# Mixing and memory attention of tokens 0 to 511 moved into the sparse units, and a fourth tile counted by ScalarE

## The chip, the cores and the metric

One core of one Trainium2 chip runs the whole kernel. The metric is the device time of one execution in microseconds (us); the number compared is the median of several executions.

## The reference, cut to what matters

One decoder layer over 1024 tokens of width 1024: a projection feeds a sparse attention (8 heads; each query keeps the 256 keys with the highest index score) and a banded attention (8 heads); their joint output is mixed with x, goes through cross attention over 256 memory tokens, and through a squared ReLU MLP, with a layer norm behind each.

```python
rel = jax.nn.relu(einsum('bthd,bsd->bths', iqb, ik))
score = einsum('bths,bth->bts', rel, iwb) * idx_scale
score = where(causal, score, -inf)
_, sel = lax.top_k(score, n_sel)             # 256 keys of each query
...
x = LN(ALPHA * x + concat(sparse, band) @ w_o)                 # mixing
x = LN(ALPHA * x + memory_cross_attention(x, mem, wq, wk, wv, wo))
x = LN(ALPHA * x + square(relu(x @ w_up)) @ w_down)            # MLP
```

## The kernel before, in words

Every fp32 product is done as three products of rounded halves: high by high, high by low, low by high (lines 651 to 653). Weights come in chunks of 128 x 2048: SP (SyncE's queue) loads a chunk into one of two buffers `raw` (L610), and POOL makes its two halves, `w_hi` (L637, four instructions of 128x512) and `w_lo` (L642, four). The program is written out by hand: each engine has its own list, and semaphores tie the lists together. In PE's order the stages are

- the projection of the values, then 28 rope halves (24 matmuls each, L651 to L653), which make queries and keys; beside halves 15 to 20 stand the index scores of tiles 2 to 7 (a tile is 128 tokens). DVE rotates each half and splits it (`roped`), ScalarE rounds and stores it;
- the band stage, 40 steps of `swa_scores`, `swa_turn` and `swa_values`, with products over the memory tokens between them (`memory_product`; the keys and values of the memory, folded into `g_dram` and `u_dram`);
- the sparse units: 48 of them, tiles 2 to 7 by 8 heads, one new unit a step. Unit d is `scores(d)` (L703, L704), two steps later `turn_probs` (L831), and one step after that `times_values` (L844). Unit d of tile i needs the key mask of tile i;
- 48 products of mixing and memory attention, g = 0 to 47, each 24 matmuls of 128x512: g 0 to 15 mixing (weights `w_o`), 16 to 31 the scores of the memory attention (weights `g_dram`), 32 to 47 its output (weights `u_dram`). The eight tiles t follow one another for each half of the columns. Behind most products the result of an earlier tile is transposed (`turn_result`, L853, 8 transposes), and DVE does the norm or the probabilities of an earlier product;
- the MLP, up and down.

The search for each tile's 256th highest score is a bisection over 31 bits. The narrow tiles 2, 3 and 4 are counted by DVE (`tally`, L1483); the three wide tiles 5, 6 and 7 by ScalarE (`count_wide`, L1047), 5 bits beside the last rope halves and the rest beside band stage and first units; then DVE makes the masks (`finish`, L1563 to L1581). `select_for(us)` lets DVE take as much of the search as a budget allows at each step.

The weights of the mixing products lie in four slots: `slot_of(c)` is `c % 2` below `C_MIX` and `(c - C_MIX) % 4` from there, so POOL converts chunk c as soon as chunk c - 4 is used. Each pair of chunks serves 8 products. `load_queries` (L528, 8 DMAs) brings the queries of a tile, three tiles at most in buffers.

Of the kernel before, what the change touches and what calls it, by code (L numbers as in the profile page):

```python
# [62 lines left out]
C_G = C_MIX + 4  # L63
C_U = C_G + 4
C_MLP = C_U + 4
# [15 lines left out]
def rope_units():  # L81

    units = [(C_K, ("k", 0), hf) for hf in range(2)]
    for chunk, what in ((C_IQ, "iq"), (C_SQ, "sq"), (C_DQ, "dq")):
        for m in range(2):
            units += [(chunk + m, (what, m), hf) for hf in range(2)]
    return units
# [6 lines left out]
INDEX_HALF = 2 * N_ROPE_INDEX + 3  # L94
BESIDE_HALF = INDEX_HALF + (NT - FIRST_TOPK_TILE)
WIDE_HALF = BESIDE_HALF + 1
# [10 lines left out]
IDX = [(i, h) for i in range(FIRST_TOPK_TILE, NT) for h in range(HEADS)]  # L107
# [26 lines left out]
L_ATT = 0  # L134
L_GEMM = L_ATT + ND
L_DOWN = L_GEMM + 3 * 2 * NT
T_SWA = 0
T_DSA = []
_n = T_SWA + NS
for _i, _h in DSA:  # L140
    T_DSA.append(_n)
    _n += (_i + 4) // 4
T_O = _n
T_STAGE = T_O + 2 * NT

N_SEL = NT - FIRST_TOPK_TILE
WIDE = N_SEL - 3
# [4 lines left out]
WIDE_END = N_HALVES - 2  # L153

def wide_bit_beside_rope(v):

    return TOP_BIT - (v - WIDE_HALF) if WIDE_HALF <= v < WIDE_END else None

def wide_bit_counted(n):

    done = WIDE_END - WIDE_HALF
    j = (4 * n + 6) // 7
    return TOP_BIT - done - j if n >= 0 and 7 * j // 4 == n and j <= TOP_BIT - done else None

MEM_STEP = 2
BUDGET_BAND, BUDGET_DSA = 1.8, 2.0
FIRST_PRODUCT = 3  # L170
# [21 lines left out]
def last_uses():  # L192
# [7 lines left out]
    for n in range(12):  # L200
        stage, ch = divmod(n // 2, 2)
        last[C_MIX + n] = ("L", L_GEMM + 16 * stage + 8 * ch + NT - 1)
# [8 lines left out]
N_GEMM = 3 * 2 * NT  # L211

def transposed_at(g):

    stage, t = divmod(g - NT - 2, 2 * NT)
    return (stage, t) if 0 <= stage < 3 and 0 <= t < NT else None

def build_layer(nc, a):  # L220
# [6 lines left out]
    with ctx:  # L227
# [9 lines left out]
        w_at = [16, 32, 80, 96]  # L237
        w_hi = [place(f"w_hi{s}", [P, CHUNK], F32R, w_at[s]) for s in range(4)]
        w_lo = [place(f"w_lo{s}", [P, CHUNK], F32R, w_at[s] + 8) for s in range(4)]
# [29 lines left out]
        act_hi = place("act_hi", [P, NT, NK, P], F32R, 112)  # L269
        act_lo = place("act_lo", [P, NT, NK, P], F32R, 144)  # L270
# [6 lines left out]
        band_prob = [place(f"band_prob{s}", [P, PAIR * BAND], F32, 183 + 2 * s) for s in range(4)]  # L277
        kv_hi = [place(f"kv_hi{s}", [P, 2, MEM], F32R, 191 + 4 * s) for s in range(2)]
        kv_lo = [place(f"kv_lo{s}", [P, 2, MEM], F32R, 193 + 4 * s) for s in range(2)]
# [18 lines left out]
        unread_wide = [place(f"unread_wide{s}", [P, SEQ], BF16, 60 + 4 * s) for s in range(3)]  # L298
# [5 lines left out]
        p_store = place("p_store", [P, NT, HALF], F32, 176.5)  # L304
        gamma = place("gamma", [P, D], F32, 192.5)
        beta = place("beta", [P, D], F32, 196.5)
        x_res = [place(f"x_res{s}", [P, HALF], F32, 200.5 + 2 * s) for s in range(2)]
        p_work = [place(f"p_work{s}", [P, HALF], F32, 200.5 + 2 * s) for s in range(2)]
# [35 lines left out]
        unread_banks = [banks[:, (2 + 2 * s) * HALF:(4 + 2 * s) * HALF] for s in range(3)]  # L344
# [58 lines left out]
        q_split = sem("q_split")  # L403
        qk_stored = sems("qk_stored", 2)
        keys_in = sem("keys_in")
# [53 lines left out]
        def raw_of(c):  # L459

            return c if c < C_MEM else c + 1

        def mem_raw(slot_view=raw[C_MEM % 2]):

            return slot_view[:].rearrange("p (k m) -> p k m", k=NK)
# [5 lines left out]
        def slot_of(c):  # L471
            return c % 2 if c < C_MIX else (c - C_MIX) % 4
# [4 lines left out]
        def source_of(c):  # L477
# [6 lines left out]
            if c < C_G:  # L484
                return a["w_o"][c - C_MIX]
            if c < C_MLP:
                dram = g_dram if c < C_U else u_dram
                ch, kh = divmod((c - C_G) % 4, 2)
                return dram[4 * kh:4 * kh + 4, :, ch * HALF:(ch + 1) * HALF].rearrange("k p n -> p k n")
# [7 lines left out]
        def _(sp):  # L497
            def load_gb(n):
                sp.dma_start(gamma[:], a["gamma"][n].partition_broadcast(P)).then_inc(gb_in, 16)
                sp.dma_start(beta[:], a["beta"][n].partition_broadcast(P)).then_inc(gb_in, 16)  # L500

            def load_queries(j):

                if j < NT - FIRST_TOPK_TILE:
                    row, i = HEAD_ROW["iq"], FIRST_TOPK_TILE + j
                    units = N_ROPE_INDEX
# [7 lines left out]
                if j >= 3:  # L514
# [6 lines left out]
                    else:  # L521
                        filled(sp, l_full, L_ATT + (before - N_BAND) * HEADS + HEADS - 1)
# [14 lines left out]
            def load_keys():  # L537

                for s in range(2):
                    sp.wait_ge(qk_stored[s], 64)  # L540
                for j in range(4):
                    for part, key in enumerate((key_hi[j], key_lo[j])):
                        for d0 in range(0, P, ROT):
                            r0 = d0 % HEAD // ROT * P + j * ROT
                            sp.dma_start(key[d0:d0 + ROT, :].bitcast(F32),
# [753 lines left out]
        def _(dve):  # L1299
# [162 lines left out]

            def select_keys():

# [523 lines left out]
```

## Time and profile before

| | |
|---|---|
| median of 3 executions | 1640.76 us (1640.23 to 1644.03) |
| the profiled execution, its time | 1633.94 us |
| its span on the core | 1632.1 us |
| mean granted clock of TensorE | 0.970 of full speed |
| PE busy, matmuls | 1513.5 us (93% of the span) |
| DVE, ScalarE, POOL busy | 892.2, 465.4, 536.1 us |

The stages by the profiled execution: projection of the values to 35.9 us, rope halves to 239.6, band stage to 452.8, sparse units to about 610, mixing and memory attention to 925, MLP to 1632.1.
### The profile page before, as it was taken

To read this page: it belongs to the slowest core of one execution; us is meant where nothing else is said; L and a number is where in the kernel's file an instruction comes from. 1 tells how busy PE (TensorE), PEld (TensorE's weight loads), DVE (VectorE), ACT (ScalarE), POOL (GpSimd) and SP (SyncE) were. 2 spreads that over 40 slices of the span, in tenths; PEclk is the share of its full clock that TensorE was granted. 3 is DMA by queue.
4 is the path that set the end of the run, shared out by engine and by line. 5 is a ranking of instruction groups with operands and counts; after the bars stand their busy time and mean duration, and the time that the engine had idled before them with its cause. 6 is when DMAs were issued, how large, how long until landed. Compare 5 with 4: busy or idle time off the path is not lost.

```text
span 1632.1 us, 20732 instructions
## 1 busy us (share of the span) xinstructions
PE 1513.5 (93%) x7720; PEld 1286.1 (79%) x7720; DVE 892.2 (55%) x1819; ACT 465.4 (29%) x987; POOL 536.1 (33%) x540
## 2 busy tenths in 40 slices
PE   7999975888768999989999999999999999999996
PEld 6887754888757998768887788888888888888884
DVE  7568986778877433593426733333333333333357
ACT  3014435788674651122211201111101011111010
POOL 5232214665510003341233153333333333333300
PEclk9999997999887999999999999999999999999998
DMA  6564223554410004211110221111111110111001
GB/s 224 178 190 149 94 100 127 179 173 151 141 46 16 12 7 168 97 42 49 52 53 0 78 78 52 52 52 52 52 52 52 52 52 29 49 52 52 1 26 78
DMA packets 61331, 128.96 MB, mean 79 GB/s; under 512 B 6960, under 2 KB 34096, under 8 KB 53552
## 3 DMA queue, kind: packets, MB, share of 16 engines
q1 hardware_dynamic: 44208, 100.37, 18.6%
q10 hardware_dynamic: 17024, 27.27, 4.7%
q8 instruction: 62, 1.02, 0.3%
q14 instruction: 37, 0.30, 0.1%
HBM read 100.35 MB, written 27.26 MB: 78 GB/s over the span
## 4 chain that ended last, share of the span: by engine, by line
PE 77%; DVE 14%; ACT 3%; issue 3%; POOL 1%; DMA 1%; ACTq 0%; SPq 0%; DVEq 0%; POOLq 0%
PE banks L651 22%; PE banks L653 22%; PE banks L652 22%; PE banks L844 3%; PE banks L703 2%; PE banks L704 2%; DVE unread L1483 2%; PE banks L831 2%; ACT unread_wide L1047 2%; PE banks L853 1%; DVE h_buf L1792 1%; DVE bn L1778 1%; PE banks L800 1%; DVE trial L1460 1%; DVE h_buf L1801 1%
## 5 line engine op out<-in xcount | busy, mean ns | idle before, releaser
L637 POOL TENSOR_SCALAR w_hi<-raw 128x512 fp32r<-128x512 f32 x268 | 174.5, 677 | 1011.9 <-PE banks L653 685.0
L642 POOL TENSOR_TENSOR w_lo<-raw,w_hi 128x512 fp32r<-128x512 f32 x268 | 363.9, 1389 | 0.0
L1892 DVE TENSOR_TENSOR h_buf<-h_buf,banks 128x1024 f32<-128x1024 f32 x112 | 136.7, 1221 | 145.8 <-PE banks L653 145.8
L651 PE MATMUL banks<-act_hi,w_hi 128*128 128x512 f32 x512 | 200.0, 391 | 1.7 <-DVE act_lo L1771 1.7
L651 PE MATMUL banks<-w_hi,hid_hi 128*128 128x512 f32 x512 | 199.3, 389 | 1.4 <-DVE hid_lo L1872 1.4
L653 PE MATMUL banks<-act_hi,w_lo 128*128 128x512 f32 x512 | 199.9, 390 | 0.0
L652 PE MATMUL banks<-act_lo,w_hi 128*128 128x512 f32 x512 | 199.7, 390 | 0.0
L653 PE MATMUL banks<-w_hi,hid_lo 128*128 128x512 f32 x512 | 199.2, 389 | 0.0
L652 PE MATMUL banks<-w_lo,hid_hi 128*128 128x512 f32 x512 | 199.2, 389 | 0.0
L1263 ACT ACTIVATE relu_buf<-banks 128x512 f32<-128x512 f32 x64 | 38.3, 599 | 523.4 <-PE banks L653 523.4
L1867 DVE TENSOR_TENSOR relu_buf<-relu_buf 128x512 f32<-128x512 f32 x64 | 45.0, 704 | 241.9 <-ACT relu_buf L1263 241.9
L651 PE MATMUL banks<-w_hi,act_hi 128*128 128x512 f32 x384 | 152.6, 397 | 0.0
L653 PE MATMUL banks<-w_hi,act_lo 128*128 128x512 f32 x384 | 150.1, 391 | 0.0
L652 PE MATMUL banks<-w_lo,act_hi 128*128 128x512 f32 x384 | 149.9, 390 | 0.0
L651 PEld LDWEIGHTS banks<-act_hi,w_hi 128*128 128x128 f32 x512 | 96.5, 189 | 22.0 <-issue 1.9
L651 PEld LDWEIGHTS banks<-w_hi,hid_hi 128*128 128x128 f32 x512 | 96.1, 188 | 21.8 <-DVE hid_lo L1872 1.9
L652 PEld LDWEIGHTS banks<-act_lo,w_hi 128*128 128x128 f32 x512 | 96.5, 189 | 20.1
L653 PEld LDWEIGHTS banks<-act_hi,w_lo 128*128 128x128 f32 x512 | 96.4, 188 | 20.1
L652 PEld LDWEIGHTS banks<-w_lo,hid_hi 128*128 128x128 f32 x512 | 96.1, 188 | 20.0
L653 PEld LDWEIGHTS banks<-w_hi,hid_lo 128*128 128x128 f32 x512 | 96.1, 188 | 20.0
L703 PE MATMUL banks<-key_hi,q_tile 128*128 128x512 f32 (+3 forms) x240 | 88.1, 374 | 23.5 <-DVE neg_max L1690 8.7
L651 PE MATMUL banks<-x_hi,w_hi 128*128 128x512 f32 x224 | 89.3, 398 | 10.0 <-DVE roped L1377 7.3
(178 smaller groups left out, 2779.6 us busy)
## 6 DMA issues: line engine op xcount, KB each, us to landing
raw<-w_up_dram SPq DMA_DIRECT2D x16, 1024.0 KB, 4.8
raw<-w_down_dram SPq DMA_DIRECT2D x16, 1024.0 KB, 4.8
q_tile<-qk_dram SPq DMA_DIRECT2D x176, 64.0 KB, 2.1
qk_dram<-q_hi ACTq DMA_DIRECT2D x28, 256.0 KB, 2.2
qk_dram<-roped ACTq DMA_DIRECT2D x28, 256.0 KB, 2.6
x_raw<-x_t_dram SPq DMA_DIRECT2D x8, 512.0 KB, 8.4
raw<-wk_mem_dram SPq DMA_DIRECT2D x4, 1024.0 KB, 5.4
raw<-wv_mem_dram SPq DMA_DIRECT2D x4, 1024.0 KB, 5.2
```

Source lines behind the costliest of these rows:

```text
L637: pool.tensor_scalar(w_hi[s][:, col], raw[r % 2][:, col], 1.0, 1.0, ALU.mult, ALU.mult)\
L642: pool.tensor_tensor(w_lo[s][:, col], raw[r % 2][:, col], w_hi[s][:, col].bitcast(F32), ALU.subtract).then_inc(w_ready, 1)
L651: pe.matmul(dst, lh, rh, start=(first and n == 0), stop=False)
L652: pe.matmul(dst, lh, rl, start=False, stop=False)
L653: last = pe.matmul(dst, ll, rh, start=False, stop=(final and n == len(parts) - 1))
L703: pe.matmul(dst[:, lo:hi], q, key_hi[key][:, k0 + lo:k0 + hi], start=True, stop=False)
L704: mm = pe.matmul(dst[:, lo:hi], q, key_lo[key][:, k0 + lo:k0 + hi], start=False, stop=True)
L831: mm = pe.transpose(ring_t[m % 2][:, (j % 4) * P:(j % 4 + 1) * P], prob[d % 2][:, j * P:(j + 1) * P], ident[:])
L844: mm = pe.matmul(ring_a[m % 2][:, h * HEAD:(h + 1) * HEAD], prob_t[d % 2][:, j * P:(j + 1) * P], v_all[:, j, HEADS:HEADS + HEAD], start=(j ...
L1263: act.activation(relu_buf[q % 2][:], ring_a[(A_UP + q) % 2][:], ACT.Relu)\
L1867: dve.tensor_tensor(relu_buf[q % 2][:], relu_buf[q % 2][:], relu_buf[q % 2][:], ALU.mult)\
L1892: dve.tensor_tensor(h_buf[:, t, :], h_buf[:, t, :], ring_l[n % 2][:], ALU.add)\
```

## The change

Tokens 0 to 511 (tiles 0 to 3, called group 0) no longer wait for the later tiles. Their 24 products stand among the steps: g0 at step 49, g1 at step 53 (in the units of tiles 2 and 3), g2 to g8 in a row at step 59, and g9 to g23 at steps 60, 62, 65, 68, 71, 74, 76, 79, 82, 85, 88, 90, 93, 94 and 94, among the units of tiles 4 to 7 (steps 60 to 91). `GAP` leaves steps 56 to 59 without a new unit. Group 1, tiles 4 to 7, has its own 24 products behind. Each pair of chunks now serves 4 products instead of 8, so the 12 chunks of weights are loaded and converted a second time for group 1 (`C_LATE`). Up to `C_LATE` the chunks have only two slots, since the sparse units hold the room of the others.

```diff
-C_G = C_MIX + 4
-C_U = C_G + 4
-C_MLP = C_U + 4
+GROUP = 4
+C_LATE = C_MIX + 12
+C_MLP = C_LATE + 12
...
+GAP = 4
+N_STEPS = NS + ND + GAP
+def unit_at(n):
+    d = n - NS
+    if d >= 2 * HEADS:
+        d = d - GAP if d >= 2 * HEADS + GAP else -1
+    return d if d < ND else -1
+def step_of_product(g):
+    if g < 2:
+        return NS + HEADS + 1 + 4 * g
+    if g < 9:
+        return NS + 2 * HEADS + 3
+    return min(NS + 2 * HEADS + GAP + 28 * (g - 9) // 10, N_STEPS + 2)
...
         def slot_of(c):
-            return c % 2 if c < C_MIX else (c - C_MIX) % 4
+            return c % 2 if c < C_LATE else (c - C_LATE + 2) % 4
...
-                if 2 <= c < C_MIX + 2:
+                if 2 <= c < C_LATE:
                     chunk_used(pool, c - 2)
-                elif C_MIX + 2 <= c < C_MIX + 4:
+                elif C_LATE <= c < C_LATE + 2:
                     attended(pool, 2 * NT - 1)
+                    chunk_used(pool, C_MIX + 9)
-                elif c >= C_MIX + 4:
+                elif c >= C_LATE + 2:
                     chunk_used(pool, c - 4)
...
-            for n in range(NS + ND + 3):
+            for n in range(N_STEPS + 3):
                 if n < NS:
                     swa_scores(n)
-                elif n < NS + ND:
-                    scores(n - NS)
+                if unit_at(n) >= 0:
+                    scores(unit_at(n))
...
+                for g in products_of_step(n):
+                    for key in first_turned(0) if g == 0 else ():
+                        turn(*key)
+                    product(0, g)
```

The selection changes too. Tile 4 is now counted by ScalarE with tiles 5 to 7, tile by tile: 6 bits beside rope halves 22 to 27, 16 in the band stage, 4 at steps 41, 46, 51 and 56, and 5 behind products g2 to g6; DVE counts tiles 2 and 3 alone. For that, index scores of tiles 2 and 3 move to halves 10 and 11 and of tiles 7, 6, 5, 4 to halves 15 to 18, and the first part of the selection of each tile is spread over halves 12, 13 and 19 to 22. POOL takes the low half (`roped` minus its rounding) of the last seven rope pairs from DVE. The memory tokens have a buffer of their own and are rounded beside the last rope half, and that half is rotated at step 2. `act_hi`, `p_store`, `gamma` and others become two buffers, one for each group.

```diff
-WIDE = N_SEL - 3
+WIDE = N_SEL - 4
...
-WIDE_HALF = BESIDE_HALF + 1
+INDEX_HALVES = {10: 2, 11: 3, 15: 7, 16: 6, 17: 5, 18: 4}
+PREPARE_HALVES = {12: 2, 13: 3, 19: 7, 20: 6, 21: 5, 22: 4}
+WIDE_HALF = 22
+POOL_SPLIT = 7
...
+COUNT_TICKS = [("step", 3 + 37 * j // N_STEP_BITS) for j in range(N_STEP_BITS)]
+COUNT_TICKS += [("step", NS + n) for n in (1, 6, 11, 16)] + [("product", g) for g in range(2, WIDE_LEFT - 18)]
...
+                if c == C_MEM:
+                    indexed(sp, i_full, len(IDX) - 1)
+                    sp.dma_start(mem_raw[:], a["mem_t"]).then_inc(mem_in, 16)
+                if C_MEM + 2 < c < C_MIX + 2:
+                    ahead = 3 + tile_at(mem_unit(c - 3) - 1)
+                else:
+                    ahead = {C_MIX + 2: NT + 6, C_MIX + 4: NT + 7, C_MIX + 6: NT + 8}.get(c, 0)
```

First place: the queue of SP about the loads of the mixing weights (a wait on `w_ready` is a wait for POOL to have converted chunk c - 2; the wait on `l_full` of a query load is one for the scores of the last unit that read the buffer). Before, all queries are ahead of the first wait for a mixing weight:

```order
L528 DMA q_tile_86<-qk_dram 32x4x128 x7
L528 DMA q_tile_84<-qk_dram 32x4x128 [waits l_full1,qk_stored1,qk_stored0]
L528 DMA q_tile_84<-qk_dram 32x4x128 x7
L499 DMA gamma<-gamma_dram 128x1024 [waits stored1,a_full1,stored0]
L500 DMA beta<-beta_dram 128x1024
L610 DMA raw_50<-w_o_dram 128x2048 [waits w_ready]
L610 DMA raw_49<-w_o_dram 128x2048 [waits w_ready]
L610 DMA raw_50<-g_dram 128x4x512 [waits w_ready]
L610 DMA raw_49<-g_dram 128x4x512 [waits w_ready]
```

After, the queries of tiles 6 and 7 stand between the weights:

```order
L739 DMA raw_49<-w_o_dram 128x2048 [waits w_ready]
L739 DMA raw_50<-w_o_dram 128x2048 [waits w_ready]
L650 DMA q_tile_86<-qk_dram 32x4x128 [waits l_full1,qk_stored1,qk_stored0]
L650 DMA q_tile_86<-qk_dram 32x4x128 x7
L739 DMA raw_49<-g_dram 128x4x512 [waits w_ready,stored1,stored0]
L739 DMA raw_50<-g_dram 128x4x512 [waits w_ready]
L650 DMA q_tile_84<-qk_dram 32x4x128 [waits l_full1,qk_stored1,qk_stored0]
L650 DMA q_tile_84<-qk_dram 32x4x128 x7
L739 DMA raw_49<-g_dram 128x4x512 [waits w_ready]
L739 DMA raw_50<-g_dram 128x4x512 [waits w_ready]
```

The query load of tile 7 (`q_tile_84`) moved between the two pairs of `g_dram` chunks; what is behind it waits until the last unit of tile 4 has its scores (unit 23, step 67).

Second place: POOL, from the last chunks of the memory products to the mixing weights. Before, two mixing chunks go into the second pair of slots, `w_hi_53` and `w_hi_54`:

```order
L637 TENSOR_SCALAR w_hi_52<-raw_49 128x512 [waits a_full1,raw_in0]
L637 TENSOR_SCALAR w_hi_52<-raw_49 128x512 x3
L642 TENSOR_TENSOR w_lo_56<-raw_49,w_hi_52 128x512 [waits w_rounded] x4
L637 TENSOR_SCALAR w_hi_53<-raw_50 128x512 [waits a_full1,raw_in1]
L637 TENSOR_SCALAR w_hi_53<-raw_50 128x512 x3
L642 TENSOR_TENSOR w_lo_57<-raw_50,w_hi_53 128x512 [waits w_rounded] x4
L637 TENSOR_SCALAR w_hi_54<-raw_49 128x512 [waits a_full1,raw_in0]
L637 TENSOR_SCALAR w_hi_54<-raw_49 128x512 x3
L642 TENSOR_TENSOR w_lo_58<-raw_49,w_hi_54 128x512 [waits w_rounded] x4
L637 TENSOR_SCALAR w_hi_51<-raw_50 128x512 [waits l_full1,raw_in1]
```

After, every pair goes to `w_hi_51` and `w_hi_52`:

```order
L775 TENSOR_SCALAR w_hi_51<-raw_49 128x512 [waits a_full1,raw_in0]
L775 TENSOR_SCALAR w_hi_51<-raw_49 128x512 x3
L780 TENSOR_TENSOR w_lo_55<-raw_49,w_hi_51 128x512 [waits w_rounded] x4
L775 TENSOR_SCALAR w_hi_52<-raw_50 128x512 [waits a_full1,raw_in1]
L775 TENSOR_SCALAR w_hi_52<-raw_50 128x512 x3
L780 TENSOR_TENSOR w_lo_56<-raw_50,w_hi_52 128x512 [waits w_rounded] x4
L775 TENSOR_SCALAR w_hi_51<-raw_49 128x512 [waits l_full1,raw_in0]
L775 TENSOR_SCALAR w_hi_51<-raw_49 128x512 x3
L780 TENSOR_TENSOR w_lo_55<-raw_49,w_hi_51 128x512 [waits w_rounded] x4
```

The conversions of a pair now name `l_full`, the end of the last product of the pair before, where in before they stood two slots ahead of it.

## Rows read from the trace of the kernel before

**Rows 1.** The page: busy time of the engines over the span.

```profile
PE 1513.5 (93%) x7720; PEld 1286.1 (79%) x7720; DVE 892.2 (55%) x1819; ACT 465.4 (29%) x987; POOL 536.1 (33%) x540
```

**Rows 2.** Busy time in stretches: stretch, length, PE, PEld, DVE, ACT, POOL, granted clock.

```profile
35.90:239.60 203.70, 190.08 (x832) 154.68 (x832) 155.98 (x265) 63.97 (x98) 58.04 (x54) 0.98 0.44 142
239.60:452.80 213.20, 166.36 (x1221) 157.52 (x1221) 165.19 (x670) 151.31 (x376) 119.69 (x129) 0.90 0.47 151
452.80:609.95 157.15, 139.46 (x998) 129.45 (x998) 90.21 (x210) 97.40 (x217) 6.80 (x8) 0.89 0.06 15
609.95:925.00 315.05, 304.54 (x1450) 251.09 (x1449) 173.58 (x317) 56.65 (x146) 93.28 (x96) 0.99 0.19 62
...
441.00:516.00 75.00, 53.81 (x285) 46.59 (x284) 63.25 (x174) 45.84 (x110) 12.79 (x14) 0.75 0.13 39
520.00:600.00 80.00, 80.00 (x636) 76.27 (x636) 31.11 (x62) 52.88 (x112) 0.00 (x0) 1.00 0.03 8
```

**Rows 3.** What PE waits for: us in total, times, longest.

```profile
PE banks L800 <- DVE h_buf L1740: 15.8, 6, 5.1
PE banks L651 <- DVE mem_lo L1661: 11.7, 1, 11.7
...
PE banks L703 <- DVE neg_max L1690: 8.7, 1, 8.7
...
PE banks L651 <- DVE roped L1377: 7.3, 2, 4.7
```

**Rows 4.** DVE's tallies of tile 4: busy, mean ns, idle before.

```profile
L1483 DVE TENSOR_SCALAR_CACHE_REDUCE unread<-score,trial,minus_rank 128x640 uint8<-128x640 f32 x31 | 29.1, 940 | 1.1
```

**Rows 5.** Chain of waits in the sparse units: start, us, what.

```profile
522.23 1.06 PE banks L844 x10
...
524.55 1.06 PE banks L844 x10
...
561.18 1.51 PE banks L844 x14
...
564.33 1.51 PE banks L844 x14
...
587.02 1.73 PE banks L844 x16
...
590.61 1.73 PE banks L844 x16
```

**Rows 6.** Timeline of POOL, one pair of chunks, its first and last group of four.

```profile
663.71 2.37 POOL L637 TENSOR_SCALAR w_hi<-raw 128x512 fp32r<-128x512 f32 x4 [27.68 <-PE banks L653]
...
673.38 5.03 POOL L642 TENSOR_TENSOR w_lo<-raw,w_hi 128x512 fp32r<-128x512 f32 x4
```

**Rows 7.** Timeline of DVE, a mixing product follows another.

```profile
669.02 0.69 DVE L1829 SCALAR_TENSOR_TENSOR h_buf<-x_res,banks 128x512 f32<-128x512 f32 x1 [4.75 <-PE banks L653]
```

**Rows 8.** Chain of waits, the eight transposes behind a product.

```profile
639.04 0.87 PE banks L853 x8
```

**Rows 9.** Timeline of SP's queue, the eight DMAs of one tile's queries.

```profile
276.02 3.71 SPq L528 DMA_DIRECT2D q_tile<-qk_dram  x8
```

**Rows 10.** DMA issues: count, KB each, us from issue to landing.

```profile
raw<-g_dram SPq DMA_DIRECT2D x4, 1024.0 KB, 5.0
```

**Rows 11.** Timeline of ScalarE, one bit of tile 5.

```profile
410.07 0.93 ACT L1047 ACTIVATE unread_wide<-score,trial 128x768 bf16<-128x768 f32 x1
```

**Rows 12.** Timeline of PE behind an idle 4.75 us.

```profile
212.61 0.63 PE L651 MATMUL banks<-x_hi,w_hi 128*128 128x512 f32 x1 [4.75 <-DVE roped L1377]
...
216.03 0.46 PE L653 MATMUL banks<-x_hi,w_lo 128*128 128x512 f32 x1
```

**Rows 13.** Timeline of DVE, a norm's first pass without and with POOL busy.

```profile
690.29 1.27 DVE L1792 SCALAR_TENSOR_TENSOR h_buf<-h_buf,mean_var,gamma 128x1024 f32<-128x1024 f32 x1
...
726.00 2.26 DVE L1792 SCALAR_TENSOR_TENSOR h_buf<-h_buf,mean_var,gamma 128x1024 f32<-128x1024 f32 x1
```

**Rows 14.** Timeline of POOL at the second of these times, the low halves of a chunk.

```profile
725.90 5.99 POOL L642 TENSOR_TENSOR w_lo<-raw,w_hi 128x512 fp32r<-128x512 f32 x4
```

## What the change does to the time: the prediction

> **What bounds the kernel now.** The page comes first: PE is busy for 93% of the span and no other engine for more than 55% [rows 1]. That is an average over stages, so the second view is the busy time in stretches [rows 2]. It shows where PE loses time. Rope halves: 13.6 us idle of 203.7. Band stage: 46.8 us idle of 213.2, clock 0.90. Sparse units: 17.7 idle of 157.15, clock 0.89. Mixing and memory attention: 10.5 idle of 315. All the losses worth having are thus between 36 and 610 us, and they are not evenly spread: from 441 to 516 PE is busy for 53.8 of 75 us and at a clock of 0.75, while DVE is busy for 63.3; from 520 to 600 PE has no idle time at all and the full clock [rows 2]. The first is where DVE finishes the search for the wide tiles; the second is the units of tiles 4 to 7, which have no gap that a product could fill.
>
> The third view is the chain of waits, for the pace of the units: from one `times_values` to the next it is 2.32 us in tile 4 (524.55 less 522.23), 3.15 in tile 6 and 3.59 in tile 7 [rows 5]; that is 0.4 a tile. Taken down by 0.4 a tile, tiles 3 and 2 would need about 1.9 and 1.5. Eight units of each tile are 8 x (1.5 + 1.9 + 2.3 + 2.7 + 3.15 + 3.6) = 121 us, against a stretch of 157: the sparse units lose 36 us to waits and to the half clock, nearly all with tiles 2 and 3. The fourth view, what PE waits for, names DVE in all the large ones: `h_buf` 15.8 us (the normalising between band tiles), `mem_lo` 11.7, `neg_max` 8.7, `roped` 7.3 [rows 3].
>
> **What the change can win.** It takes work from DVE where PE waits for it.
>
> Rope halves: the index scores' tail and the first part of the selection are spread, and POOL splits the later pairs. I count the two waits for `roped`, 7.3 us [rows 3]; at least 0, at most the whole idle 13.6.
>
> Band stage: the memory is rounded and split beside the last rope half (the wait for `mem_lo`, 11.7, and behind it `neg_max`, 8.7, which was the first mask operation, late by the same work), and tile 4's 31 tallies, 29.1 us of DVE, leave DVE [rows 3, 4]. Of the 15.8 us for `h_buf` I count 9, since DVE has still tiles 2 and 3 to count. That is 29.4; at least the 11.7, at most 50 (idle time and some of the half clock).
>
> Sparse units: tiles 2 and 3 now run while ScalarE still counts, so the masks of the wide tiles are no longer what holds DVE there. What holds them is ScalarE: it is busy for 52.9 of the 80 us from 520 to 600 [rows 2], in which some 28 units pass, 1.9 us for each at 640 to 1024 columns; for 384 and 512 columns I take 1.4. To the 16 units come four bits. One bit of tile 5 takes 0.93 us for 768 columns [rows 11], so the 3328 columns of four tiles take 4.0; 16 x 1.4 + 4 x 4.0 = 38 us beside 27 us of PE's own (8 x 1.5 + 8 x 1.9), in which g0 and g1 (10.9 us) also fit. So some 12 of the 36 us stay and 24 are won; at least 0, at most 36.
>
> Sum of what is won: 7.3 + 29.4 + 24 = 60.7 us.
>
> **What the change costs.** Products and units give PE the same matmuls as before. The weights don't: 12 chunks more are made by POOL, and up to `C_LATE` in two slots. The conversion of a pair can't start before the last product on the pair before has ended, and the product's first matmul waits for the whole pair. A pair takes POOL from 663.71 to 678.41 (673.38 and 5.03), 14.7 us [rows 6]. Before, each pair had two slots of its own and eight products' time of 43.5 us. Now PE has, between the last product of a pair and the first of the next, only this (a product is 4.75 + 0.69 = 5.44 us [rows 7], eight transposes 0.87 [rows 8]):
>
> g4, behind g3 in the row: nothing. Wait 14.7.
> g8, in the same row: one turn. 14.7 - 0.87 = 13.8.
> g12: its raw chunks are loaded behind the queries of tile 7, and those wait for the scores of unit 23 in step 67. Eight DMA issues 3.7 us [rows 9], landing of the weights 5.0 [rows 10], the pair 14.7, less what PE has left of steps 67 and 68, 4.0 (the rest of one unit of tile 4 and 5 each): 19.4.
> g16: three units of tile 6 and a turn, 3 x 3.15 + 0.87: 4.4.
> g20: two units of tile 7, 2 x 3.59: 7.5.
> First product of group 1: its slots come free with the last unit, and g22, g23 and two turns lie beside: 14.7 - 10.9 - 1.7 = 2.1.
>
> Together 61.9 us. The bounds: if the raw chunk or the queries came earlier the g12 term would be at 14.7 - 4.0 = 10.7; and if DVE is what PE would wait for anyway, a wait for weights in the same place costs nothing (below).
>
> Each of the first five stops also costs clock. Behind 4.75 us without work, PE issued 8 matmuls in 3.42 us (212.61 to 216.03) where 8 at full clock take 8 x 5.44 / 24 = 1.8 [rows 12]: 1.6 us a restart, 5 x 1.6 = 8.0. The Trainium skill, "TensorE: Matmul & The Clock Gate", section "HAM oscillation — how this bites in real kernels", says that a gap makes the stretch behind it begin in the throttled state; the trace agrees with rows 12, and that speaks against a schedule with more gaps.
>
> The last term is DVE. In group 0 the norms and the memory softmax come in the same stretch as the masks for tiles 4 to 7, and POOL converts for longer beside them. The trace has no row for this mix. From below it is 0 (the stops for weights hide it). From above: the stretch with the masks, 441 to 516, lost 21.2 us idle and, at 0.75 with 53.8 busy, about 13 to the clock, 34 in all [rows 2], and it would move here unchanged. The masks of tile 5 to 7 can be spread over steps 60 to 83, so only that of tile 4 is due at once, while the norms have pieces of their own that PE waits for; I take half, 18.
>
> Sum of costs: 61.9 + 8.0 + 18 = 87.9. The MLP is unchanged. Net: +27.2 us. The profiled execution has 1633.9 us (span 1632.1), so its counterpart would be at 1661; the median of the runs lies 6.8 above the profiled execution, and I carry that over: 1668 us.
>
> **The rivals.** *Faster.* One mechanism: DVE was late all through the band stage because of tile 4's 29.1 us [rows 4], so without them all 50 us of loss there go instead of 29, and the masks and norms fall wholly inside the stops for weights. Then 27.2 - 21 - 18 = -12, or 1629. For it: DVE is the releaser in every large wait [rows 3]. Against it: ScalarE takes a fourth tile, 22 bits of 0.8 us (640 columns at the rate of the tile 5 row) more up to the end of the band stage, where it is already busy for 151 of 213 us [rows 2]. It decides where the costs fall under 61 us in all.
>
> *No change.* Gains and costs level at some 65 to 75 us: 1641.
>
> *Slower still: DVE and POOL hold each other.* POOL now works beside the norms in group 0 and for the 12 extra chunks. With POOL busy a norm's pass took 2.26 us instead of 1.27 [rows 13], and POOL's own low halves 5.99 instead of 5.03 [rows 6, 14]; with the high halves that is some 9.3 a chunk against 7.4, or 3.8 more a pair. Six pairs are 23 us on the path, and two passes for each of eight norms 16 more, of which half on the path: 31, so 1699. The Trainium skill, "SBUF — State Buffer", section "SBUF: two separate sides", has the two engines lock each other out of a shared port; rows 13 agree in size (1.8 times as long), and by a full lock the pair would be as long as all DVE work beside it added, which here is this same rival.
>
> *Not what it says.* That units and products would not overlap at all is what the costs above already describe for g4 and g8; apart from those each product has units around it.
>
> **Chances.** Forecast (net cost of some 10 to 50 us) 0.64; faster, with 1629, 0.14; level 0.07; the contention rival 0.15. A measurement of this kernel can tell 0.3% from no change, 1636 to 1646. So faster 0.14, same 0.07, slower 0.79. The range is from 1636, the edge of faster, to 1702, just above the contention rival: it leaves out 0.14 below and about 0.06 above. The likeliest case alone is at 1652 to 1686.
>
> **What would show it.** In the waits of PE, `w_lo` of POOL becomes the largest: six stops, of about 15, 14, 19, 4, 7 and 2 us, five of them in a stretch that began with g4. POOL starts a pair right at the end of g3, g7, g15 and g19, but for g12 only after the queries and the landing. `mem_lo` goes from the waits, and `h_buf` falls to about 7. The stretch of tiles 2 and 3 has PE at over 70% busy. In the MLP nothing changes, 707 us. The prediction is wrong if the stops for weights are short because PE is late for another reason at those places (masks, norms, counts), if the band stage loses under 5 us, or if the row g2 to g8 waits longer for norms than for weights.

## The result, and the profile after

The change makes the kernel slower: 1734.79 us (1732.80 to 1737.63, 4 runs) against 1641.17 (1640.23 to 1644.03), a ratio of 1.0569 with a 95% interval of 1.0546 to 1.0591. The prediction had said 1668, with 1636 to 1702 as its range. The profiled execution took 1732.96 us, 99 more than that of before.

The page of after, its first lines (compare [rows 1]):

```profile
span 1731.1 us, 20937 instructions
...
PE 1546.3 (89%) x7720; PEld 1312.3 (76%) x7720; DVE 886.5 (51%) x1759; ACT 495.7 (29%) x1053; POOL 653.6 (38%) x650
```

PE has the same 7720 matmuls, but is busy 32.8 us longer (the same work at a lower mean granted clock, 0.942 against 0.970) and idle 66.2 us longer (184.8 against 118.6). The busy time in stretches, columns as in [rows 2], shows where:

```profile
35.90:230.00 194.10, 183.94 (x809) 150.56 (x810) 148.29 (x246) 67.06 (x106) 69.97 (x65) 0.98 0.45 146
230.00:433.00 203.00, 179.08 (x1288) 169.77 (x1287) 153.79 (x616) 158.01 (x401) 132.62 (x140) 0.93 0.52 165
433.00:510.00 77.00, 60.58 (x309) 52.51 (x308) 24.47 (x76) 38.42 (x88) 0.88 (x1) 0.80 0.21 72
510.00:598.00 88.00, 50.10 (x204) 39.66 (x203) 49.55 (x116) 25.69 (x54) 30.94 (x32) 0.77 0.10 33
598.00:800.00 202.00, 158.31 (x932) 138.69 (x933) 77.25 (x139) 67.92 (x157) 44.04 (x48) 0.85 0.14 46
800.00:1024.00 224.00, 201.33 (x962) 167.80 (x960) 125.33 (x212) 42.42 (x97) 116.69 (x112) 0.95 0.24 82
1024.00:1731.10 707.10, 688.88 (x3034) 569.38 (x3032) 280.34 (x332) 81.72 (x138) 241.92 (x240) 0.99 0.15 52
```

These edges are round numbers; the stages are told apart by what PE does. The first scores of tile 2 are the first matmul with 384 columns, here in before and in after:

```profile
452.80 0.42 PE L703 MATMUL banks<-key_hi,q_tile 128*128 128x384 f32 x1
```

```profile
427.61 0.42 PE L843 MATMUL banks<-key_hi,q_tile 128*128 128x384 f32 x1
```

So the rope halves and the band stage are 25.2 us shorter. The MLP takes 707.1 us in both. What lies between, units and products, is this in before and in after:

```profile
452.80:924.07 471.27, 443.06 (x2438) 379.75 (x2438) 263.79 (x527) 153.31 (x361) 100.09 (x104) 0.96 0.14 46
```

```profile
427.61:1023.10 595.49, 474.81 (x2439) 402.92 (x2439) 279.12 (x549) 178.31 (x404) 197.94 (x199) 0.87 0.18 61
```

124.2 us are lost there, 92.5 of them idle time of PE (120.7 against 28.2) and 31.8 more busy time.

What PE waits for in after, columns as in [rows 3]:

```profile
PE banks L789 <- POOL w_lo L780: 60.6, 7, 19.1
PE banks L997 <- DVE act_lo L1896: 19.5, 9, 7.5
PE banks L843 <- issue: 10.7, 4, 5.8
...
PE banks L975 <- DVE act_lo L1896: 7.3, 6, 2.1
...
PE banks L789 <- DVE mem_lo L1802: 4.7, 1, 4.7
PE banks L944 <- DVE h_buf L1885: 4.7, 3, 2.1
```

The weights now lead. The timelines of PE and POOL in after show the first stop, before g4:

```profile
516.38 0.39 PE L791 MATMUL banks<-w_hi,act_lo 128*128 128x512 f32 x1
531.47 0.79 PE L789 MATMUL banks<-w_hi,act_hi 128*128 128x512 f32 x1 [14.71 <-POOL w_lo L780]
532.06 0.63 PE L790 MATMUL banks<-w_lo,act_hi 128*128 128x512 f32 x1
```

```profile
516.93 2.37 POOL L775 TENSOR_SCALAR w_hi<-raw 128x512 fp32r<-128x512 f32 x4 [83.05 <-PE banks L791]
519.26 4.93 POOL L780 TENSOR_TENSOR w_lo<-raw,w_hi 128x512 fp32r<-128x512 f32 x4
524.15 2.38 POOL L775 TENSOR_SCALAR w_hi<-raw 128x512 fp32r<-128x512 f32 x4
```

POOL has been idle for 83 us with the raw chunks in place, starts when g3 ends, and PE, which has nothing else in its row, waits for exactly the pair. The second place where PE has long waits is that of the masks of tiles 4 and 5, behind g9; the timelines of PE and of DVE:

```profile
598.29 0.77 PE L843 MATMUL banks<-key_hi,q_tile 128*128 128x512 f32 x1 [5.80 <-issue]
...
602.71 0.76 PE L843 MATMUL banks<-key_hi,q_tile 128*128 128x512 f32 x1 [2.90 <-issue]
...
609.80 0.77 PE L789 MATMUL banks<-w_hi,act_hi 128*128 128x512 f32 x1 [4.03 <-DVE neg_max L1852]
```

```profile
596.83 0.49 DVE L1730 TENSOR_SCALAR score<-score 128x640 f32<-128x640 f32 x1
...
608.22 0.56 DVE L1730 TENSOR_SCALAR score<-score 128x768 f32<-128x768 f32 x1
608.82 0.82 DVE L1852 CUSTOM_DVE_ANT_0 logit<-banks,score 128x640 f32<-128x640 f32 x1
```

The first DVE row ends the mask of tile 4 (640 columns). The second ends that of tile 5 (768 columns), and the third, which serves a unit of tile 4, stood behind it. For the first two waits the profile names no releaser; DVE has no idle time up to 602.3.

### The profile page after: what moved, and what is told of

Read it like the earlier page. It is cut to its first block, busy times and chain, and to the rows that moved or that the text cites. A ratio compares the mean times of both kernels' runs of the same rounds, so it can differ in the third digit from the quotient of the medians.

```text
span 1731.1 us, 20937 instructions
## 1 busy us (share of the span) xinstructions
PE 1546.3 (89%) x7720; PEld 1312.3 (76%) x7720; DVE 886.5 (51%) x1759; ACT 495.7 (29%) x1053; POOL 653.6 (38%) x650
## 4 chain that ended last, share of the span: by engine, by line
PE 48%; DVE 4%; issue 1%; ACT 0%; POOL 0%; ACTq 0%; DVEq 0%
PE banks L789 16%; PE banks L790 16%; PE banks L791 16%; DVE h_buf L1918 1%; PE banks L997 1%; DVE bn L1903 1%; PE banks L988 0%; DVE act_lo L1896 0%; DVE h_buf L1927 0%; DVE newton L1923 0%; DVE h_buf L2076 0%; DVE rstd L1926 0%; ACT act_hi L1346 0%; DVE h_buf L1955 0%; PE banks L975 0%
## 5 line engine op out<-in xcount | busy, mean ns | idle before, releaser
L775 POOL TENSOR_SCALAR w_hi<-raw 128x512 fp32r<-128x512 f32 x316 | 207.6, 684 | 917.5 <-PE banks L791 768.2
L780 POOL TENSOR_TENSOR w_lo<-raw,w_hi 128x512 fp32r<-128x512 f32 x316 | 430.6, 1394 | 0.0
L789 PE MATMUL banks<-w_hi,act_hi 128*128 128x512 f32 x384 | 163.3, 425 | 66.3 <-POOL w_lo L780 57.4
L790 PE MATMUL banks<-w_lo,act_hi 128*128 128x512 f32 x384 | 158.6, 413 | 0.0
L791 PE MATMUL banks<-w_hi,act_lo 128*128 128x512 f32 x384 | 157.7, 411 | 0.0
L789 PEld LDWEIGHTS banks<-w_hi,act_hi 128*128 128x128 f32 x384 | 78.3, 204 | 84.2 <-POOL w_lo L780 58.5
L843 PE MATMUL banks<-key_hi,q_tile 128*128 128x512 f32 (+3 forms) x240 | 88.6, 376 | 17.4 <-issue 10.7
```

The source lines that it names most:

```text
L775: pool.tensor_scalar(w_hi[s][:, col], raw[c % 2][:, col], 1.0, 1.0, ALU.mult, ALU.mult)\
L780: pool.tensor_tensor(w_lo[s][:, col], raw[c % 2][:, col], w_hi[s][:, col].bitcast(F32), ALU.subtract).then_inc(w_ready, 1)
L789: pe.matmul(dst, lh, rh, start=(first and n == 0), stop=False)
L790: pe.matmul(dst, lh, rl, start=False, stop=False)
L791: last = pe.matmul(dst, ll, rh, start=False, stop=(final and n == len(parts) - 1))
L843: pe.matmul(dst[:, lo:hi], q, key_hi[key][:, k0 + lo:k0 + hi], start=True, stop=False)
```

## The experiments

Ratios are to the kernel before on the same chip; after is at 1.0569.

**POOL converts almost nothing for group 0.** The pairs behind the first are rounded for 32 columns of each quarter only, so the weights are mostly old ones.

```diff
+                def cols(p):
+                    w = n // PIECES if not C_MIX + 2 <= c < C_LATE else 32
+                    return slice(p * n // PIECES, p * n // PIECES + w)
```

> POOL rounds only 32 of 512 columns of each quarter of the ten chunks behind the first pair of group 0, so the products of group 0 run on mostly old weights; loads, waits and products stay. Theory A (the stops for POOL are real path time, 57 us idle in the trace of after plus the half clock behind them): the time falls from 1735 by about 55 to 68 us, to 1667 to 1680, and the waits for w_lo in group 0 fall below 8 us, all at g12 for the landing. Theory B (PE would wait at these places anyway, for norms, counts and masks): the waits move to DVE and the time stays above 1710.

Measured: 1682.51 us, ratio 1.0304 (1.0268 to 1.0339). That is 0.0265 or 43 us less. What PE waits for there:

```profile
PE banks L793 <- POOL w_lo L784: 16.1, 5, 9.7
```

The waits for `w_lo` fell by 44.5 us in all (60.6 to 16.1) and the time by about as much: the waits left over are the short conversions and, at g12, 9.7 us for the landing. A microsecond taken out of the stops is about a microsecond of the kernel. Theory A's range was missed: the stops weren't emptied. Theory B falls. The edit also takes work off POOL beside DVE, so it isn't a test of the waits alone; the next run and the one with the products in fours leave POOL its work.

**The queries of tile 7 two chunks later on SP.**

```diff
-                    ahead = {C_MIX + 2: NT + 6, C_MIX + 4: NT + 7, C_MIX + 6: NT + 8}.get(c, 0)
+                    ahead = {C_MIX + 2: NT + 6, C_MIX + 4: NT + 7, C_MIX + 8: NT + 8}.get(c, 0)
```

> The queries of tile 7 are loaded two chunks later on SP. Theory A: the stop before g12 falls from 19.1 us to about 10 (a pair, 14.7, less the units of steps 66 to 68 which lie beside, some 7), the time to 1724 to 1728. Theory B: masks and exp hold PE there too, no change beyond 2 us.

Measured: 1722.07 us, ratio 1.0527 (1.0493 to 1.0561), 0.0042 or 7 us less; in its trace the stop before g12 is 7.1 us instead of 19.1, and that of g16, 1.5 in after, is 3.1. The interval touches that of after, so the size rests on the traces. In after the SP and POOL timelines read:

```profile
639.28 3.64 SPq L650 DMA_DIRECT2D q_tile<-qk_dram  x8
642.97 0.98 SPq L739 DMA_DIRECT2D raw<-g_dram  x2
```

```profile
648.38 2.37 POOL L775 TENSOR_SCALAR w_hi<-raw 128x512 fp32r<-128x512 f32 x4 [73.13 <-DMA raw<-g_dram]
650.71 4.92 POOL L780 TENSOR_TENSOR w_lo<-raw,w_hi 128x512 fp32r<-128x512 f32 x4
```

The chunks are issued right behind the queries, and POOL waits for them to land.

**The last nine bits counted over 32 columns.** The kept keys are others.

```diff
+                    w = (i + 1) * P if TOP_BIT - k < N_EARLY + N_STEP_BITS else 32
-                    act.activation(dst[:, 0:(i + 1) * P], score[i][:], ACT.Sign,
+                    act.activation(dst[:, 0:w], score[i][:, 0:w], ACT.Sign,
```

> The last nine bits of the four wide tiles are counted over 32 columns instead of 640 to 1024, so the kept keys are others; the number of instructions and waits stays. Theory A: ScalarE's 4.0 us a bit is what holds PE among tiles 2 and 3 at four places (steps 41, 46, 51, 56), together some 12 to 16 us, and the five behind g2 to g6 lie in the stops; time 1719 to 1724. Rival: the band stage end, DVE's steps and the half clock are what holds, so less than 5 us.

Measured: 1707.41 us, ratio 1.0455 (1.0419 to 1.0491), 0.0114 or 19 us less, more than the 12 to 16 expected. In its trace g3 starts at 488.2 instead of 509.55, 21.4 of the 24.1 us by which the two profiled executions differ, and the stops behind it are as long as in after. So the four bits among tiles 2 and 3 cost nearly all of it. From the first scores of tile 2 to the first matmul of g2, in after and then here:

```profile
427.61:498.74 71.13, 57.15 (x318) 50.41 (x318) 23.98 (x78) 40.37 (x94) 6.27 (x7) 0.81 0.23 78
```

```profile
427.65:479.11 51.46, 46.66 (x318) 41.08 (x317) 22.63 (x78) 29.76 (x94) 6.49 (x7) 0.97 0.31 106
```

Both have the same 318 matmuls. Of the 19.7 us between them 9.2 are idle time of PE and 10.5 are busy time, at a granted clock of 0.81 against 0.97. One of the bits in after, on ScalarE:

```profile
446.51 1.14 ACT L1196 ACTIVATE unread_late<-score,trial 128x1024 bf16<-128x1024 f32 x1
...
447.64 1.03 ACT L1196 ACTIVATE unread_late<-score,trial 128x896 bf16<-128x896 f32 x1
...
448.67 0.93 ACT L1196 ACTIVATE unread_late<-score,trial 128x768 bf16<-128x768 f32 x1
...
449.59 0.82 ACT L1196 ACTIVATE unread_late<-score,trial 128x640 bf16<-128x640 f32 x1
```

From 446.51 to the next `exp` at 450.40 ScalarE does nothing for the units: 3.9 us.

**Both at once.** Short conversions and short counts.

> After without two of its costs at once: short conversions for group 0, as in the run without conversion (1.0304), and the last nine bits counted over 32 columns, as in the run with short counts (1.0455). Theory: the two costs lie in different places, the counts that matter among tiles 2 and 3 and the stops behind them, so the gains add: 1.0569 less 0.0265 less 0.0114 is 1.019. Rival: the five counts behind g2 to g6 come up as a wait once the stops are gone, and the gain together is larger than the sum: 1.008 to 1.013.

Measured: 1659.55 us, ratio 1.0138 (1.0097 to 1.0178), 0.0431 less; the sum of the two single gains is 0.0379. With intervals of 0.004 each the two readings can't be told apart; the gains add, as far as this can tell. The 23 us that stay above before have other causes.

**The stops filled with matmuls that nothing reads.**

```diff
-                pe.wait_ge(w_ready, PIECES * (c + 1))
...
+                if grp == 0:
+                    for _ in range({4: 52, 8: 48, 12: 66, 20: 24}.get(g, 0)):
+                        pe.matmul(ring_l[n % 2][:, HALF:2 * HALF], act_hi[0][:, t, 0, :],
+                                  act_hi[0][:, t, 0:4, :], start=True, stop=True)
+                pe.wait_ge(w_ready, PIECES * (c + 1))
```

> After, with matmuls of 128x512 on data already there, into a part of the bank that nothing reads, ahead of the wait for weights: 52 before g4, 48 before g8, 66 before g12, 24 before g20, at 0.227 us each a little shorter than the stops of 14.7, 14.45, 19.1 and 7.6 us. Nothing that POOL does changes. Theory: the half clock behind a stop is a cost of its own, 1.8 to 2.8 us in the product behind it (7.4 to 8.4 instead of 5.7) and some more in the units behind; time 8 to 14 us under that of after, ratio to before 1.048 to 1.052. Rival: what PE does slower behind a stop is hidden by the waits for DVE and ScalarE that come next, change under 4 us.

Measured: 1731.12 us, ratio 1.0584 (1.0549 to 1.0618): no gain. At g4 the matmuls kept the clock up: compare the line at 531.47 in after with this one, from the timeline of the filled kernel. At g12 they didn't, as the last row shows:

```profile
535.94 0.50 PE L789 MATMUL banks<-w_hi,act_hi 128*128 128x512 f32 x1 [3.07 <-POOL w_lo L780]
536.28 0.40 PE L790 MATMUL banks<-w_lo,act_hi 128*128 128x512 f32 x1
...
664.75 0.79 PE L789 MATMUL banks<-w_hi,act_hi 128*128 128x512 f32 x1 [4.86 <-POOL w_lo L780]
```

The fill left 3.1, 3.7, 4.9 and 2.2 us of the four stops idle. g4 took 5.8 us instead of 8.2, but g8 7.4 instead of 8.4, g12 8.5 instead of 7.4 and g20 7.3 instead of 7.9: 2.9 us for the four together. From g4 to g8 2.3 us were saved in the trace, from g8 to g9 1.0; but from g9 to g10, where PE waits for masks, it took as long as in after (23.9 us), the stretch from g11 to g12 was 0.8 us longer, and between g14 and g15 3.2 us were lost to something that this one trace doesn't explain. So the expected 8 to 14 us are not there, but the run tests little of the half clock, since it took little of it away. What the half clock behind the stops costs the kernel is not shown.

**Products in fours, five units between fours.** The nine late bits all come at steps 41 to 56.

```diff
-    if g < 2:
-        return NS + HEADS + 1 + 4 * g
-    if g < 9:
-        return NS + 2 * HEADS + 3
-    return min(NS + 2 * HEADS + GAP + 28 * (g - 9) // 10, N_STEPS + 2)
+    return NS + [9, 13, 19, 19, 25, 25, 26, 26, 31, 31, 32, 32,
+                 37, 37, 38, 38, 43, 43, 44, 44, 49, 51, 54, 54][g]
...
-COUNT_TICKS += [("step", NS + n) for n in (1, 6, 11, 16)] + [("product", g) for g in range(2, WIDE_LEFT - 18)]
+COUNT_TICKS += [("step", NS + n) for n in (1, 3, 5, 7, 9, 11, 13, 15, 16)]
```

> The products of group 0 stand in fours: g0 step 49, g1 53, g2 and g3 59, g4 to g7 steps 65 and 66, g8 to g11 71 and 72, g12 to g15 77 and 78, g16 to g19 83 and 84, g20 89, g21 91, g22 and g23 94, with five units between fours; the nine late bits all stand at steps 41 to 56. Theory A: stops for w_lo in group 0 fall from 57 us to under 8 and the clock stays up, against it one bit more or so in every second unit of tiles 2 and 3 (5 bits, up to 20 us); time 1680 to 1700. Theory B: 1720 or more.

Measured: 1690.69 us, ratio 1.0342 (1.0302 to 1.0382). PE's waits for `w_lo` are down to 3.1 us in all, with the very same work for POOL: the units cover a conversion if five of them stand in front of it. The gain is 37 us and not 57. Part of the rest goes to the five more bits among tiles 2 and 3: from the first scores of tile 2 to g2 the trace has 79.3 us instead of 71.1. Another part goes to one line that I had not expected, in the timeline of DVE:

```profile
785.76 20.42 DVE L1915 SCALAR_TENSOR_TENSOR h_buf<-h_buf,mean_var,gamma 128x1024 f32<-128x1024 f32 x1
806.11 0.21 DVE L1920 SCALAR_TENSOR_TENSOR newton<-rstd,var_eps 128x1 f32<-128x1 f32 x1
```

It takes 1.27 us elsewhere [rows 13]. POOL at the same time, four chunks without a pause, the last row ending at 805.10:

```profile
785.62 5.05 POOL L777 TENSOR_TENSOR w_lo<-raw,w_hi 128x512 fp32r<-128x512 f32 x4
790.60 2.40 POOL L772 TENSOR_SCALAR w_hi<-raw 128x512 fp32r<-128x512 f32 x4
792.93 4.96 POOL L777 TENSOR_TENSOR w_lo<-raw,w_hi 128x512 fp32r<-128x512 f32 x4
797.82 2.40 POOL L772 TENSOR_SCALAR w_hi<-raw 128x512 fp32r<-128x512 f32 x4
800.14 4.96 POOL L777 TENSOR_TENSOR w_lo<-raw,w_hi 128x512 fp32r<-128x512 f32 x4
```

**The same, and POOL pauses after two chunks until DVE's norms are done.**

```diff
                 elif c >= C_LATE + 2:
                     chunk_used(pool, c - 4)
+                    if c == C_LATE + 2:
+                        pool.wait_ge(ln_done, 2 * GROUP)
```

> The kernel with the products in fours, and POOL waits ahead of the third chunk of group 1 until the eighth norm of group 0 is done. In the run before, one DVE norm pass lasted 20.4 us from 785.76, to the end of four chunks that POOL made without a pause. Theory: POOL holds DVE off there for as long as it has work; with the pause after two chunks (790.6) the pass ends at about 792, and the time falls by about 14 us, ratio to before 1.024 to 1.028. Rival: that pass was late for another reason (gamma, a semaphore, one odd execution), and the pause gives nothing or makes the later conversion late: 0 to +8 us.

Measured: 1678.91 us, ratio 1.0262 (1.0237 to 1.0287), 0.0080 or 13 us less, as expected of the theory that POOL held DVE off. The four executions without the pause lie 12.5 us apart, 1683.66 to 1696.18, and the profiled one is the longest of them; those with the pause lie 2.4 us apart. In its trace the same norm pass:

```profile
783.67 2.23 DVE L1917 SCALAR_TENSOR_TENSOR h_buf<-h_buf,mean_var,gamma 128x1024 f32<-128x1024 f32 x1
```

It overlapped the low halves of the second chunk (783.53 to 789.50) and got in between its instructions, so being held off for a whole burst isn't what always happens; the profile shows one execution.

**All products of group 0 behind the units.** The rest of the change stays; the weights have four slots as in before. The nine late bits now all come at steps 40 to 54, among tiles 2 and 3, where after had four.

```diff
-GAP = 4
+GAP = 0
...
+    return N_STEPS + 2
...
-COUNT_TICKS += [("step", NS + n) for n in (1, 6, 11, 16)] + [("product", g) for g in range(2, WIDE_LEFT - 18)]
+COUNT_TICKS += [("step", NS + n) for n in (0, 2, 4, 6, 8, 10, 12, 13, 14)]
...
-            return c % 2 if c < C_LATE else (c - C_LATE + 2) % 4
+            return c % 2 if c < C_MIX + 2 else (c - C_MIX) % 4
```

> Only the other half of the change: selection, rope order, POOL split, four tiles counted by ScalarE and the two groups of products stay, but all 24 products of group 0 stand behind the last unit, with four slots for their weights as in before; the nine late bits are at steps 40 to 54. Theory: the interleaving is what costs; rope and band stage keep their gain of 20 us, the units cost as in before (157 us) within 10, two groups instead of one cost a norm's tail, some 8 us; time 1620 to 1640, ratio 0.993 to 1.003. Rival: counting a fourth tile on ScalarE and masks late cost more than DVE gives back: ratio 1.01 or more.

Measured: 1657.23 us, ratio 1.0128 (1.0097 to 1.0158). The interleaving, with its two slots, makes 0.044 or 72 us of the 94. But 21 us stay, which my theory had not expected; the ratio is that of the rival. In its trace the units start at 427.58, 25.2 us earlier than in before, and end at 601.7 instead of 609.95: they take 174.2 us instead of 157.2, 17 more. Among tiles 2 and 3 PE waits 10.1 us in all for `prob`, what ScalarE's `exp` writes, and behind the mask of tile 4 it waits 6.1. The larger loss is in the products: from 601.7 to the first turns for the MLP at 947.7, where before had 609.95 to 924.1, 32 us more. The timeline of PE at the first of them:

```profile
601.74 1.04 PE L992 MATMUL banks<-ident,h_buf 128*128 128x128 f32 x8
604.56 0.56 PE L784 MATMUL banks<-w_hi,act_hi 128*128 128x512 f32 x1 [1.78 <-DVE act_lo L1891]
604.92 0.63 PE L785 MATMUL banks<-w_lo,act_hi 128*128 128x512 f32 x1
```

Group 0 turns a tile right ahead of its product (`first_turned(0)` has one tile), where before had turned two; PE waits 1.8 to 2.4 us before each of the first four and runs three of them in 7.1 to 7.3 us instead of 5.7.

**The same, with tiles turned two ahead.**

```diff
-    return [(0, GROUP * grp + t) for t in range(grp + 1)]
+    return [(0, GROUP * grp + t) for t in range(2)]
...
-    out = [(0, GROUP * grp + g + grp + 1)] if g + grp + 1 < GROUP else []
+    out = [(0, GROUP * grp + g + 2)] if g + 2 < GROUP else []
```

> The kernel with all products of group 0 behind the units (1.0128 of before), and its first tiles are turned two ahead of their product, as in before, instead of one. Theory: one tile ahead leaves PE without work for 2.4 us before each of the first four products, at 7.1 to 7.3 us instead of 5.7 for each; the time falls by 10 to 15 us, ratio 1.004 to 1.007. Rival: those gaps are filled again by waits for DVE's norms, under 4 us.

Measured: 1643.93 us, ratio 1.0040 (1.0021 to 1.0058), 0.0088 or 14 us less, as expected.

**And the border between the groups bridged.** Tiles 4 and 5 are turned behind g20 and g21.

```diff
-    return [(0, GROUP * grp + t) for t in range(2)]
+    return [(0, GROUP * grp + t) for t in range(0 if grp else 2)]
...
+    if grp == 0 and 20 <= g < 22:
+        out.append((0, GROUP + g - 20))
```

> The same, and the first two tiles of group 1 are turned behind g20 and g21 of group 0, ahead of the norm that DVE does between the groups. Theory: the border between the groups costs a wait of 8.1 us, two of 1.8 and slow products, some 15 us in all; the ratio falls by 0.006 to 0.009 more, to 0.995 to 1.000. Rival: DVE's norms are late at the border anyway and the wait moves behind the first products of group 1: no change.

Measured: 1643.83 us, ratio 1.0038 (1.0019 to 1.0056): no change. Its timeline of PE around the border, two rows:

```profile
761.13 1.16 PE L994 MATMUL banks<-ident,h_buf 128*128 128x128 f32 x8 [2.74 <-DVE act_lo L1893]
769.59 1.73 PE L994 MATMUL banks<-ident,h_buf 128*128 128x128 f32 x7 [7.29 <-DVE act_lo L1893]
```

The wait of 8.1 us at the border became 7.3 one product later, since DVE's norms are what is late there. The rival holds. **With the products in fours, bridged behind g22 and g23** (same edit, other numbers):

> The kernel with the products of group 0 in fours among the units and with POOL's pause (1.0262), and the first two tiles of group 1 turned behind g22 and g23. Theory: the border costs here what it costs with the products behind; ratio 1.018 to 1.022. Rival: here POOL's pair, which the first product waits for, hides it: no change.

Measured: 1678.42 us, ratio 1.0253 (1.0228 to 1.0277), no change to 1.0262 either. **Four of the late bits moved into the band stage** (`N_STEP_BITS = 20`), in the bridged kernel:

> The kernel with products behind, two ahead and bridged, and 20 instead of 16 bits counted in the band stage, 5 instead of 9 among the units of tiles 2 and 3. Theory: among tiles 2 and 3 ScalarE is what ends the waits, 4.0 us a bit, in the band stage it has room (158 of 203 us busy): 6 to 14 us less, ratio 0.988 to 0.996. Rival: the band stage is as full, counting there delays its exp and move, and nothing is won.

Measured: 1643.40 us, ratio 1.0036 (1.0021 to 1.0051): no change. In its trace the first turn behind the units starts at 603.15, in the bridged kernel at 598.46. The first scores of tile 2 stand at 434.29 and 424.36: the units became 5.2 us shorter (168.9 against 174.1), and what lies ahead of them 9.9 us longer. So the band stage had no room for the bits, as the rival has it; this is one execution of each.

## Why the prediction was wrong

The side was right and the mechanism it named first was right; the size was 67 us short, 72 by the profiled executions: 11.5 in what was won ahead of the units, 60 behind. By its steps:

- **Stops for weights, 61.9 us.** Right: 14.71, 14.45, 19.09, 1.52 and 7.63 us in the trace, 57.4, against 14.7, 13.8, 19.4, 4.4 and 7.5. g16's was shorter since waits for `act_lo` lay in front of it. The run without conversion shows that they are path time, and the later queries and the fours show their cause. The figures for g4, g8, g12 and g20 were within 0.7 us.
- **Sparse units, 24 us won.** This is the step that failed. I had laid ScalarE's 38 us beside PE's 27 and let only the difference, some 12, stay of the 36 lost; g0 and g1 were to fit in besides. Even with g0 and g1 on top the stretch from the first scores of tile 2 to g2 would then be 27 + 12 + 10.9, some 50 us. It took 71.1, and with the bits short 51.5. So four bits cost 20 us in the trace and 19 by the runs, and of the 24 hardly any were won. I had added up ScalarE's work and called it parallel to PE's; but a unit's `exp` stands in line behind a bit, and PE stands in line behind that `exp`, so the bits come on top, half as idle time and half as a lower clock. The working also contradicts itself: if g0 and g1 fit into the 38 us, PE has no idle time left in them, and no 12 can stay.
- **Group 1's start, 2.1 us.** I had looked at the weights alone. g23 ends at 841.5 and the first product starts at 855.9: 14.4 us, a wait of 7.5 for `act_lo` in it, since DVE has the norms of tiles 2 and 3 to do before it splits tile 4. The two bridged runs show that the order of the turns isn't the cause; DVE's norms are due there in any order, an argument from where the wait went, not shown by a run without norms.
- **Turning one tile ahead.** The order showed it and I gave it no term. It costs 14 us with the products behind; how much in after wasn't tried, but its waits for `act_lo` of 1.8, 1.3, 1.3 and 2.4 us from g0 to g3 are there.
- **Rope halves and band stage, 36.7 us won.** Mis-sized: 25.2. `mem_lo` fell from 11.7 to 4.7 rather than to 0, `h_buf` from 15.8 to 4.7 and `roped` from 7.3 to 2.5, better than I had counted; against it stand waits for ScalarE (`stage_out` 3.7 instead of 1.3) and DVE passes held up by POOL's split: `roped<-roped,rot_part` at 1.73 to 1.77 us instead of 0.69 at five places.
- **Half clock, 8.0 us.** The products behind the five stops took 39.2 us instead of five times 5.7, 10.7 more, so the size was about right for PE. Whether that is path time is open: the filled stops gave no gain, but gave back only 2.9 us of it. The term left out the places without a stop: among tiles 2 and 3 the lower clock makes 10.5 us. The Trainium skill, "TensorE: Matmul & The Clock Gate", section "HAM oscillation — how this bites in real kernels", has a gap followed by slow work; the trace agrees (8.2 us for g4, 5.8 filled).
- **DVE in the row, 18 us; contention, a rival at 1699.** The first was about right: PE waits 5.8 us behind the mask of tile 4 and 2.9 and 4.0 around the parts of that of tile 5, 12.7 in all, and 3 us for norms. The second didn't occur in the form that I priced: of the pairs of group 0 only that of g8 was held up, 16.5 us (558.80 to 575.26) instead of 14.7. The pair for group 1's first product took 19.6 us, but was ready 6.6 us ahead of it. It came in one of my own schedules, larger than I had thought for one place.

Of the 94 us, runs account for 43 (stops) and 19 (late bits), and with both gone 1.0138 is left, some 23 us, although what lies ahead of the units is shorter than in before: the border, the turns and the masks of tiles 4 and 5. How these divide isn't settled. No version tried is faster than before; the nearest three, with the products behind and two tiles ahead, are 0.4% slower. In the trace of the first of them 26.3 us are won ahead of the units, 17.1 lost in the units and 18.4 in the products.

## What to carry to other kernels

When work is moved, look at the buffers that feed it as well as at the engine it fills: with one pair of slots, each change of weights is a full stop of the production time, 14.7 us here, unless that much other work stands between the last use and the next; the same products in fours had 3 us of stops. When one engine stands between two others (PE, `exp` on ScalarE, PE), work put on it in between can be added to the chain in full, however idle it is on average: four counts of 3.9 us cost 19 here. And splitting a long run of products in groups repeats its ends: the first turns and the last norm are exposed once for each group, 13 to 14 us from the last product of the one to the first of the other here.

## What the runs showed of the hardware

A DVE pass with two SBUF inputs took 20.42 us instead of 1.27 and ended 1.1 us after POOL's burst of four chunks; a pause in the burst took 13 us off the kernel. In the trace with the pause, a pass beside the burst took 2.23. The Trainium skill, "SBUF — State Buffer", section "SBUF: two separate sides", says that the loser of the shared port pair blocks for the other's whole instruction. That fits the 2.2 us. The 20.4 us is the rest of four chunks, many POOL instructions on end, more than one instruction's lock explains, and one profiled execution shows it. Also new to me: of the 20 us that four bits on ScalarE cost, PE's idle time was only half; the same 318 matmuls took 57.2 us at a granted clock of 0.81 and 46.7 at 0.97.
